# Ten norm products in another order, and a scratch tile moved from PSUM to SBUF, in the latent-attention norm of a two-block transformer

## The reference, cut to what matters

```python
qa = (rms_norm_2(c_q, q_a_norm[l]) @ w_uq[l]).reshape(B, S, MLA_HEADS, MLA_QK)
qa = rms_norm_2(qa, mla_q_norm[l])
qa = jnp.concatenate([qa[..., :MLA_NOPE], rope(qa[..., MLA_NOPE:], positions)], axis=-1)
kv = (rms_norm_2(c_kv, kv_a_norm[l]) @ w_ukv[l]).reshape(B, S, MLA_HEADS, MLA_NOPE + MLA_V)
k_nope, va = kv[..., :MLA_NOPE], kv[..., MLA_NOPE:]
k_pe_h = jnp.broadcast_to(k_pe[:, :, None, :], (B, S, MLA_HEADS, MLA_ROPE))
ka = rms_norm_2(jnp.concatenate([k_nope, k_pe_h], axis=-1), mla_k_norm[l])
ka = jnp.concatenate([ka[..., :MLA_NOPE], rope(ka[..., MLA_NOPE:], positions)], axis=-1)
o_a = mla_attention(qa, ka, va)
```

## Time and profile before

| | us |
|---|---|
| median of three runs (lowest, highest) | 4080.72 (4080.56, 4082.0) |
| the profiled execution | 4080.72 |
| its span in the profile | 4078.9 |
| PE busy in the span | 3819.6 |
| DVE, ACT, POOL busy | 1880.8, 1480.2, 1612.1 |
| granted PE clock, mean | 0.975 of full |

### The profile page before, as it was taken

One profiled execution on the slowest core, in us unless ns is written; L12 is line 12 of the kernel. 1 busy time (PEld: TensorE's weight loads), 2 busy tenths in 40 slices (PEclk: granted clock), 3 DMA queues, 4 the chain that ended last, 5 costly groups with the idle time before them and its releaser, 6 DMA issues. The chain is left out here.

```text
span 4078.9 us, 52392 instructions
## 1 busy us (share of the span) xinstructions
PE 3819.6 (94%) x19218; PEld 3029.9 (74%) x19218; DVE 1880.8 (46%) x3264; ACT 1480.2 (36%) x2293; POOL 1612.1 (40%) x801
## 2 busy tenths in 40 slices
PE   6987899999898899999999899999999999899999
PEld 5875688888675668887888754788878877547887
DVE  2675866543636565654554846222232222452222
ACT  3264532222335663333222545322232223543222
POOL 1321243444330036554554421455555553115554
PEclk8999999999999999999999999999999999999999
DMA  7610134442110026663765210233323332102332
GB/s 249 194 37 19 58 114 135 144 138 62 42 47 19 1 72 219 216 216 95 230 222 184 69 58 10 64 97 98 93 83 98 97 89 73 42 1 83 99 99 76
DMA packets 460502, 411.96 MB, mean 101 GB/s; under 512 B 28095, under 2 KB 405311, under 8 KB 460351
## 3 DMA queue, kind: packets, MB, share of 16 engines
q1 hardware_dynamic: 457903, 408.65, 32.5%
q10 hardware_dynamic: 2448, 1.32, 0.1%
HBM read 406.25 MB, written 7.60 MB: 101 GB/s over the span
## 5 line engine op out<-in xcount | busy, mean ns | idle before, releaser
L222 POOL TENSOR_TENSOR s_wlo<-s_raw,s_whi 128x1024 fp32r<-128x1024 f32 x490 | 1180.3, 2417 | 1929.0 <-ACT s_whi L214 1927.5
L236 PE MATMUL psum<-s_xhi,s_whi 128*128 128x512 f32 x3264 | 1228.0, 376 | 20.8 <-POOL s_wlo L222 11.2
L237 PE MATMUL psum<-s_xlo,s_whi 128*128 128x512 f32 x3264 | 1220.0, 374 | 0.0
L238 PE MATMUL psum<-s_xhi,s_wlo 128*128 128x512 f32 x3264 | 1217.1, 373 | 0.0
L214 ACT ACTIVATE s_whi<-s_raw 128x1024 fp32r<-128x1024 f32 x490 | 510.1, 1056 | 1535.3 <-PE psum L238 1530.8
L236 PEld LDWEIGHTS psum<-s_xhi,s_whi 128*128 128x128 f32 x3264 | 616.1, 189 | 140.0 <-POOL s_wlo L222 13.6
L237 PEld LDWEIGHTS psum<-s_xlo,s_whi 128*128 128x128 f32 x3264 | 616.0, 189 | 111.5 <-issue 3.6
L238 PEld LDWEIGHTS psum<-s_xhi,s_wlo 128*128 128x128 f32 x3264 | 614.7, 188 | 112.0
L236 PE MATMUL psum<-s_ahi,s_whi 128*128 128x512 f32 x1232 | 469.1, 381 | 11.6 <-DVE s_y L1309 7.2
L238 PE MATMUL psum<-s_ahi,s_wlo 128*128 128x512 f32 x1232 | 464.9, 377 | 0.0
L237 PE MATMUL psum<-s_alo,s_whi 128*128 128x512 f32 x1232 | 462.4, 375 | 0.0
(11 more groups left out here) (306 smaller groups left out, 4245.4 us busy)
## 6 DMA issues: line engine op xcount, KB each, us to landing
s_ada_raw<-w_ada SPq DMA_DIRECT2D x224, 512.0 KB, 3.9
s_raw<-w_gu SPq DMA_DIRECT2D x176, 512.0 KB, 3.8
s_raw<-w_up SPq DMA_DIRECT2D x88, 512.0 KB, 4.7
s_raw<-w_dn SPq DMA_DIRECT2D x88, 512.0 KB, 3.5
s_raw<-w_down SPq DMA_DIRECT2D x44, 512.0 KB, 4.6
s_raw<-w_in SPq DMA_DIRECT2D x30, 512.0 KB, 3.9
s_raw<-w_in_ab SPq DMA_DIRECT2D x20, 512.0 KB, 6.6
s_area<-w_first SPq DMA_DIRECT2D x16, 512.0 KB, 11.9
```

What stands on the lines that cost most here:

```text
L222: pool.tensor_tensor(K.wlo[:, c % HL, 0:a * b], K.raw[:, c % RAW, 0:a * b], K.whi[:, c % HL, 0:a * b].bitcast(F32), ALU.subtract).then_inc ...
L236: pe.matmul(out, lh, rh, start=first, stop=False)
L237: pe.matmul(out, lh, rl, start=False, stop=False)
L238: return pe.matmul(out, ll, rh, start=False, stop=last)
```

## The change

Two edits in `MlaNorm`. The list that sets the order of the ten products, and of the ten DVE multiplications that follow it, is written in another order. And the scratch tile of the Newton step is no longer the sums' own PSUM bank but `self.tmp`, which is `at(5120, TX)[0:96]`, 96 by 512 in SBUF; the argument was already passed and not used.

```diff
-        self.spread = [("qn", 0), ("qn", 1), ("qn", 2), ("kn", 0), ("kn", 1), ("kn", 2), ("qp", 0), ("qp", 1),
-                       ("kp", 0), ("kp", 1)]
+        self.spread = [("qn", 0), ("kn", 0), ("qp", 0), ("kp", 0), ("qn", 1), ("kn", 1), ("qn", 2), ("kn", 2),
+                       ("qp", 1), ("kp", 1)]
         super().__init__(K)
...
-        total, r, tmp = self.sums(), K.rstd[0:96, 0:TX], self.sums()
+        total, r, tmp = self.sums(), K.rstd[0:96, 0:TX], self.tmp
         e.scalar_tensor_tensor(out=tmp, in0=total, scalar=96 * EPS, in1=r, op0=ALU.add, op1=ALU.mult).then_inc(K.sem["dve_step"], 1)
```

## The result

| | before | changed |
|---|---|---|
| median, us (lowest to highest of five runs) | 4082.0 (4080.56 to 4082.59) | 4103.48 (4100.53 to 4104.47) |
| ratio to before, 95% interval | | 1.0053 (1.0038 to 1.0067) |
| the profiled execution, its span | 4080.72, 4078.9 | 4102.06, 4100.3 |

What follows compares the result with a forecast made beforehand. DVE's ten multiplications, ahead of the attention's scores, were taken to bound the changed phase. Per MlaNorm 1.85 + 1.86 + 6.9 + 0.75 = 11.4, twice 22.7, on 4080.7 gives 4103.4 us; 8-in-10 range 4092 to 4110.

Steps and rivals of the forecast that it cites:

- part two: New order of the ten products: PE sets the pace, 9.10 us from its start to the end against 7.24.
- DVE and POOL take turns: Newton step, lines 2572 and 2574: DVE with two SBUF inputs waits for POOL's instructions; ten start 1.85 us later.
- the order, at the full clock: Ten products: neighbours on the same rows can't run side by side on PE; 1.86 us more per MlaNorm.
- the low clock on the ten: Ten products: longer PE idle and lone narrow products bring the clock's fall 0.7 us into them; costs 6.9.
- the attention: First scores behind the ten, before at the full clock, now run at the low one: 0.75 us more.
- five places: Run of six 32-row products: only kn 1 and qn 2 overlap, leaving five places, 4.49 us.
- The clock does not fall sooner: Rival, ten products: only the direct terms stay, 2 x 3.7 = 7.4 us, total 4088; chance 0.12.
- PE packs the ten whatever their order: Rival, ten products: DVE stays the pace, only turn-taking costs, 2 x 1.85 = 3.7 us, 4084; chance 0.07.
- Not slower: Rival, attention's start: earlier fall is over by the scores, giving back the low stretch; -2.2 us, 4078.5; chance 0.03.

Runs made afterwards that it cites:

- order alone: Kernel before with only the new order of the ten products, scratch tile left in PSUM: 4087.93 us, ratio 1.0018.
- Holding POOL back: Changed kernel with POOL's five subtractions waiting until line 2574 is done: 4088.09 us, ratio 1.0017.
- the idle filled: Ten more hold matmuls before the ten products: with the scratch tile in SBUF and old order 4086.41 us; in the changed kernel 4091.64.
- three arrangements: Kernel before plus holds: five behind the ten, 4081.22 us; ten ordered by shape, holds between and behind, 4087.72; five behind plus attention holds, 4083.32.
- the list with equal rows side by side: Kernel before, scratch tile in PSUM, 32-row products listed qn 0, kn 0, qn 1, kn 1, qn 2, kn 2: 4083.98 us, single run.
- the first two kernels with holds behind the ten: Kernel before with five holds behind the ten, 4081.22 us; and with the ten ordered by shape, four holds between shapes, five behind, 4087.72.

## Why the prediction was right, step by step

The time (4103.4 forecast, 4103.48 measured), the sign and the mechanism were right. One step was wrong, the number of places in part two, and it hardly moved the end. All four terms measured a little under their forecasts, 1.9 us in the sum of both mixers. That the total still fits to 0.1 has another source: the median of before was 4082.0 beside this result and not 4080.7 (1.3), and the rest of the program took some 0.6 longer. Per mixer, us:

| step | forecast | measured | from |
|---|---|---|---|
| DVE and POOL take turns | 1.85 | 1.78 | line 2570's start to line 2574's end: 3.92 for 2.14 |
| the order, at the full clock | 1.86 | 1.69 | order alone, second mixer |
| the low clock on the ten | 6.9 | 6.43 | the rest of the 9.90 up to the scores |
| the attention | 0.75 | 0.47, 0.51 | first to last score |
| both mixers | 22.7 | 20.8 | |
| the whole | 22.7 | 21.3 | the profiled executions, 4102.06 and 4080.72 |

- *The turn-taking* came as worked out from the one case in the trace of before: 1.53 and 1.65 for lines 2572 and 2574 (forecast 1.51 and 1.73), each ending 0.55 behind POOL. The trace agrees with the Trainium skill's exclusive lock (SBUF — State Buffer, "Who interferes with whom") as far as who waits for whom; what stands behind the release is 0.55, not the instruction's whole 0.69. Holding POOL back removed it.
- *The order.* That neighbours on the same rows follow each other at 0.86, and that a change of shape costs 1.05, held: in the order-alone kernel's second mixer, at the full clock, the two weight loads of `kn` 0 stand 0.43 apart (3606.03 and 3606.46), each pair on equal rows takes 1.91 up to the next shape (3605.50, 3607.41, 3609.32), and the last multiplication ended 8.91 behind PE's start (forecast 9.10). The step that failed is "only `kn` 1 and `qn` 2 are neighbours on different rows and share a place, so five places". There were four. The weight loads of the changed kernel in that run of six:

```profile
2515.08 0.51 PEld L2520 LDWEIGHTS psum<-s_rstd,s_area 32*128 32x128 f32 x4 [1.50 <-issue]
2516.10 0.34 PEld L2520 LDWEIGHTS psum<-s_rstd,s_area 32*128 32x128 f32 x2 [0.51 <-issue]
2516.95 0.34 PEld L2520 LDWEIGHTS psum<-s_rstd,s_area 32*128 32x128 f32 x2 [0.51 <-issue]
2517.82 0.33 PEld L2520 LDWEIGHTS psum<-s_rstd,s_area 32*128 32x128 f32 x1 [0.52 <-issue]
```

`qn` 2 began with `qn` 1, past `kn` 1, and `kn` 2 with `kn` 1. DVE still took the results in the list's order: `kn` 1 at 2518.90, `qn` 2 at 2519.50. That saved PE a place of 0.86, but behind `kn` 1 four multiplications then stood in a row at DVE, at 0.60 each, so at the full clock the end moved by 0.2 only.
- *The clock* was the largest term and was right for the reason given: the fall came at 2507.3, 0.4 ahead of the ten (forecast 0.7 into them), and low products cost 1.71 and 2.0 for 0.86 and 1.05. PE's stretch of ten products grew from 7.53 (order alone, second mixer) to 14.62, by 7.09, where the forecast had 7.5 on five places with all of it low. But at the full clock DVE's last multiplication started 0.70 behind PE's end, because of the row of four, and at the low clock 0.03 behind; so 0.67 of the 7.09 did not reach the end. That is why 6.43. The split by experiment, each against its own set's before: with the idle filled, 7.8 us of 11.4 came back with the old order, and 11.7 of 21.5 in the changed kernel. The idle is not the only cause: with it filled in the changed kernel the clock fell 3.1 us into the lone narrow products, and with the order alone, at the old idle of 0.63, 2.2 us into them in one mixer.
- *The attention's first scores* ran low as forecast; 0.3 less was lost than 0.75, since the scores and what follows had 11.4 and 11.5 us at the low clock in place of 10.2, and not the 1.6 more that 0.84 us of work take there.
- *The rivals.* "The clock does not fall sooner" is what filling the idle produces, 4086 with the old order; it is not what the change does. "PE packs the ten whatever their order" was half right: it packs across rows, not across products on the same rows. "Not slower" did not occur; its chance leaned in part on rows 10, where no low stretch is shorter than 6.8 us, but the trace of before has shorter ones elsewhere (3.4 us from 1103.6).

Where it was too sure: the same kernel spreads over 16 us from run to run in the larger sets. The order-alone trace, with a fall inside the ten in one mixer and behind them in the other, shows one source of such a spread. The closeness of 4103.4 to 4103.5 is luck; that the three large steps lie within a tenth of their forecasts (the attention's is a third low) is not.

## What to carry to other kernels

Before a scratch tile moves from PSUM to SBUF, look at what POOL does beside it: an instruction that costs the same alone can double. And price a short new PE idle, or a change from packed to single narrow products, by the clock that follows it and not by its own length: 3.5 us of direct cost per mixer became 10.4. Wide filler matmuls paid in the idle that the changes had made (7.8 and 11.7 us); put into the kernel before, in three arrangements, they moved or shortened the fall and gained nothing in the total.

## What the runs showed of the hardware that was not expected

In these traces PE started float32 products of a 32-row slice past others in front of them in program order whose rows were in use: `qn` 2 past `kn` 1 in the changed kernel, and in the list with equal rows side by side `qn` 1 past `kn` 0 and `qn` 2 past `kn` 0 and `kn` 1. The readers still took the results in program order. This did not reach across shapes: 64-row and 32-row products overlapped in no trace here, 1.05 us each at the full clock and 2.0 at the low one. And the clock's low stretches are not tied to one place of the program: in the first two kernels with holds behind the ten, 10.2 us at the low clock appeared 13 us later in three mixers of four and cost as much or more (37.42 and 37.50 for 35.5), and in the fourth only 3.4 us did.
